# Two more pairs as seven block products in two feed-forward networks, small filler products and another GpSimd order at the head

## The chip, the cores and the metric

The kernel runs on one core of one Trainium2 chip. The metric is the device time of one execution in microseconds (us). The page of the profile names the engines of the core by short names: PE is TensorE, which multiplies matrices (PEld is its loading of weights), DVE is VectorE, ACT is ScalarE, POOL is GpSimd, and SP is the engine that does little but start transfers.

## What is computed

The reference is a trunk of two layers on 512 tokens of width 1024. Each layer is a feed-forward network, an attention mixer and a second feed-forward network, each behind a normalisation that is shifted, scaled and gated by columns computed from a conditioning vector `c`:

```python
for i in range(DEPTH):                      # 2
    mod = silu(c) @ mod_w[i] + mod_b[i]     # nine vectors of 1024
    sh1, sc1, g1, sh2, sc2, g2, sh3, sc3, g3 = jnp.split(mod, 9, axis=-1)
    h = modulate(rms_norm(x), sh1, sc1)
    x = x + 0.5 * g1[:, None, :] * swiglu(h, ffn1_w_gu[i], ffn1_w_down[i])
    h = modulate(rms_norm(x), sh2, sc2)
    x = x + g2[:, None, :] * mixer(h)       # sparse attention, then forgetting attention
    h = modulate(rms_norm(x), sh3, sc3)
    x = x + 0.5 * g3[:, None, :] * swiglu(h, ffn2_w_gu[i], ffn2_w_down[i])
    x = rms_norm(x, post_gain[i])
```

`swiglu` multiplies `h` by a gate matrix and an up matrix of 1024 x 2816, forms `silu(gate) * up`, and multiplies by a down matrix. All of it is float32.

## The kernel before

**Tiles.** The 512 tokens lie along the free dimension, the features on partitions. A weight matrix comes as units of 128 output features: one unit is a tile of 128 x 1024 (8 blocks of 128 x 128). Each unit is loaded by SP into one of four slots of `wraw`, split by ACT into a rounded part `whi` (line 664 or 675) and by DVE into the rest `wlo` (line 1125 or 1131), and multiplied by TensorE in three products: `whi` by the rounded activations, `wlo` by the rounded ones, `whi` by their rest. 

**The four networks.** They are numbered f = 0 to 3. A network goes in three thirds of 8, 8 and 6 pairs. A pair is a gate unit and an up unit of the same 128 hidden features; after the pairs of a third come 8 down units. A **plain pair** is 2 units x 8 blocks x 3 products = 48 matmuls of 512 columns (lines 1862, 1863, 1867). A **summed pair** takes the 2 x 2 blocks of the two units and of the activations and forms seven block products instead of eight: 7 x 4 blocks x 3 products = 84 matmuls of 256 columns (lines 1942 to 1944, `sum_pair` on PE). `PLAIN_PAIRS` says how many pairs of each third stay plain; all others are summed.

**What a summed pair asks of the other engines.** DVE adds and subtracts the weight blocks in `combine` (lines 1149 to 1154) for the pair that comes next, splits its four groups (`group_lo`, line 1131), and puts the partial sums together (lines 1192, 1195, 1201). ACT rounds the groups (`group_hi`, line 675) and copies partial sums out of PSUM before TensorE writes the bank again: `keep_one` (line 702), and in `sum_pair` the two, five and three (lines 719, 721, 724). TensorE's seventh product waits for the copy of line 724 (`three_kept`). On ACT that copy stands behind the rounding of group 1 of the next pair, and this rounding waits for the third of the four instructions of DVE's `combine` for that pair (line 1152).

**Before the first summed pair of a network** DVE also forms four differences of the activations (`diff_t`, line 1166), which ACT rounds and DVE splits (`split_t`, line 1172); `T_ROUND_AT` and `T_SPLIT_AT` say after which plain pair. In network 2 DVE also scales the result of layer 0 in eight instructions (`post_first`, line 1463), placed by `POSTS_AT`; they read a PSUM bank that the summed pairs use, so TensorE waits for all eight (`pe.wait_ge(posted, KT)`) ahead of the first summed pair.

**The columns.** `mod` is computed on DVE, one tile of 128 x 1024 at a time (`mod_column`, line 1215). `MOD_PLACES` lists for each network after which pair (third, 0, pair) or which down unit (third, 1, unit) a tile is done. GpSimd fetches the tiles into a few slots (`fetch`, `late_place`).

**Order.** There is no scheduler. Each engine runs its instructions in the order in which its block of the program issues them, and waits on counters. On DVE the loop over the plain pairs of a network issues, for pair n: the product of gate and up (line 1486), the split of the weights of pair n + 2, or, if that is the first summed pair, its `combine` and two groups, the rest of the hidden tile (line 1498), then what the tables place there: the splits of the differences, the columns, the scalings. DVE's `sum_pair` begins with the `combine` of the next pair.

**The head.** TensorE spreads the conditioning vector (line 2134), sums squares (line 2138) and spreads the root (line 1952), with waits in between, in `first_stat`. Then `first_units` multiplies the first four units, block by block, as DVE (line 1609), ACT (lines 776 and 779) and GpSimd (line 561) finish each of the 8 blocks of the normalised activations: for each block units 0 and 1, then units 2 and 3 of the block before. GpSimd also splits the weights of units 2 and 3 (`first_lo`, line 553).

## Time and profile before

| | |
|---|---|
| median of 3 runs | 1936.67 us (1932.82 to 1937.36) |
| the profiled execution | 1936.46 us |
| its span in the trace | 1934.7 us |
| PE busy | 1903.3 us (98%) |
| DVE busy | 1508.9 us (78%) |
| ACT busy | 967.6 us (50%) |
| POOL busy | 212.5 us (11%) |

The span is the time from the first to the last instruction of the program; 1.8 us of the execution lie around it. PE's busy time counts matmuls that overlap each other in the pipeline, so it does not tell how fast they follow one another; the starts of the instructions do. A row of the timeline begins with its start and its duration in us; where instructions of one kind follow without a gap they are merged, and xN gives their number. In square brackets stands how long the engine had been idle before and what ended it. The granted clock (PEclk) is 1.00 at 2.4 GHz and 0.50 at 1.2 GHz.

### The profile page before, as it was taken

How to read it: one execution, taken by the hardware profiler on the slowest of the kernel's cores; microseconds unless marked ns; L12 is line 12 of the kernel's file. 1: busy time of each engine (PE TensorE's matmuls, PEld its weight loads, DVE VectorE, ACT ScalarE, POOL GpSimd, SP SyncE). 2: the span in 40 equal slices, each digit the busy share in tenths (PEclk: the TensorE clock that was granted, in tenths of full speed). 3: DMA queues.
4: the chain of work that ended last, by engine and by line, in shares of the span. 5: the costliest groups of instructions: out<-in, count | busy, mean ns of one | idle time of the engine just before them, and what ended most of it. 6: DMA issues, size and time to landing. Idle time of an engine off the chain costs nothing.

```text
span 1934.7 us, 29256 instructions
## 1 busy us (share of the span) xinstructions
PE 1903.3 (98%) x11364; PEld 1690.3 (87%) x11364; DVE 1508.9 (78%) x2264; ACT 967.6 (50%) x1556; POOL 212.5 (11%) x245
## 2 busy tenths in 40 slices
PE   6999999999999999999999999999999999999998
PEld 5789989888888889899888999977888889899897
DVE  7889888699868798897888988785555478578485
ACT  5324626464746436346542653655565456356264
POOL 3110000016710020000011000001101000000000
PEclk9999999999999999999999999999999999999999
DMA  8775352322053583633267443323223232323232
GB/s 336 275 277 188 123 174 92 119 88 88 23 163 120 187 287 115 224 110 103 80 207 258 164 147 116 109 88 115 88 91 95 61 98 83 125 87 120 77 101 75
DMA packets 76411, 264.84 MB, mean 137 GB/s; under 512 B 8897, under 2 KB 11073, under 8 KB 76274
## 3 DMA queue, kind: packets, MB, share of 16 engines
q1 hardware_dynamic: 55296, 190.34, 30.3%
q0 software_dynamic: 20256, 72.02, 10.8%
q8 instruction: 91, 1.49, 0.3%
q10 hardware_dynamic: 722, 0.61, 0.1%
q14 instruction: 46, 0.38, 0.1%
HBM read 260.66 MB, written 2.13 MB: 136 GB/s over the span
## 4 chain that ended last, share of the span: by engine, by line
PE 88%; DVE 7%; issue 1%; DMA 1%; POOL 1%; ACT 1%; SPq 0%; DVEq 0%; ACTq 0%; POOLq 0%
PE bank L1862 17%; PE bank L1867 16%; PE bank L1863 16%; PE bank L1943 11%; PE bank L1942 11%; PE bank L1944 11%; DVE arena L1679 1%; DVE arena L1215 1%; DVE top L1678 1%; PE bank L2348 1%; PE bank L2365 1%; PE bank L2280 1%; PE bank L2124 1%; DVE h_lo L1395 1%; DVE wlo L1125 1%
## 5 line engine op out<-in xcount | busy, mean ns | idle before, releaser
L1862 PE MATMUL bank<-hid_hi,whi 128*128 128x512 f32 (+1 forms) x856 | 328.8, 384 | 0.0
L1863 PE MATMUL bank<-hid_hi,wlo 128*128 128x512 f32 (+1 forms) x856 | 328.0, 383 | 0.0
L1867 PE MATMUL bank<-hid_lo,whi 128*128 128x512 f32 (+1 forms) x856 | 328.0, 383 | 0.0
L1862 PE MATMUL bank<-h_hi,whi 128*128 128x512 f32 x784 | 313.4, 400 | 5.2 <-ACT h_hi L779 2.8
L1863 PE MATMUL bank<-h_hi,wlo 128*128 128x512 f32 x784 | 307.1, 392 | 0.0
L664 ACT ACTIVATE whi<-wraw 128x1024 fp32r<-128x1024 f32 x210 | 219.4, 1053 | 150.1 <-PE bank L1867 129.6
L1942 PE MATMUL bank<-h_hi,whi 128*128 128x256 f32 x1024 | 289.9, 283 | 0.5 <-ACT sq L724 0.5
L1943 PE MATMUL bank<-h_hi,wlo 128*128 128x256 f32 x1024 | 289.7, 283 | 0.0
L1944 PE MATMUL bank<-h_lo,whi 128*128 128x256 f32 x1024 | 289.7, 283 | 0.0
L1125 DVE TENSOR_TENSOR wlo<-wraw,whi 128x1024 fp32r<-128x1024 f32 x196 | 238.2, 1223 | 58.6 <-ACT whi L664 58.2
L1867 PE MATMUL bank<-h_lo,whi 128*128 128x512 f32 x784 | 279.4, 393 | 3.1 <-POOL h_lo L561 3.0
L1943 PE MATMUL bank<-mix,wlo 128*128 128x256 f32 x768 | 217.2, 283 | 0.0
L1944 PE MATMUL bank<-mix,whi 128*128 128x256 f32 x768 | 217.0, 283 | 0.0
L1942 PE MATMUL bank<-mix,whi 128*128 128x256 f32 x768 | 215.5, 281 | 0.0
L675 ACT ACTIVATE whi<-arena 128x1024 fp32r<-128x1024 f32 x128 | 135.2, 1056 | 137.9 <-PE bank L1944 56.1
L1131 DVE TENSOR_TENSOR wlo<-arena,whi 128x1024 fp32r<-128x1024 f32 x128 | 156.6, 1224 | 54.1 <-ACT whi L675 53.8
L1942 PEld LDWEIGHTS bank<-h_hi,whi 128*128 128x128 f32 x1024 | 196.3, 192 | 1.5 <-ACT sq L724 0.7
L1943 PEld LDWEIGHTS bank<-h_hi,wlo 128*128 128x128 f32 x1024 | 196.2, 192 | 0.4
L1944 PEld LDWEIGHTS bank<-h_lo,whi 128*128 128x128 f32 x1024 | 196.3, 192 | 0.0
L1867 PEld LDWEIGHTS bank<-hid_lo,whi 128*128 128x128 f32 x856 | 160.8, 188 | 31.7
L1862 PEld LDWEIGHTS bank<-hid_hi,whi 128*128 128x128 f32 x856 | 160.9, 188 | 31.0
L1863 PEld LDWEIGHTS bank<-hid_hi,wlo 128*128 128x128 f32 x856 | 160.9, 188 | 30.9
(294 smaller groups left out, 3353.7 us busy)
## 6 DMA issues: line engine op xcount, KB each, us to landing
wraw<-in_w_units_dram SPq DMA_DIRECT2D x306, 512.0 KB, 3.8
arena<-in_mod_t_dram POOLq DMA_DIRECT2D x96, 512.0 KB, 5.2
mod_tile<-in_mod_t_dram POOLq DMA_DIRECT2D x32, 512.0 KB, 5.5
wraw<-in_w_units_dram SPq DMA_DIRECT2D x32, 384.0 KB, 3.2
arena<-in_w_units_dram SPq DMA_DIRECT2D x10, 512.0 KB, 4.3
arena<-in_mod_t_dram SPq DMA_DIRECT2D x7, 512.0 KB, 5.9
xT<-in_xt_dram SPq DMA_DIRECT2D x8, 256.0 KB, 4.2
sq<-k_roots POOLq DMA_DIRECT2D x8, 256.0 KB, 3.7
```

The lines of the kernel that those rows point to most:

```text
L664: act.activation(whi[:, s % RING, :, :], wraw[:, s % RING, :, :], ACT.Copy).then_inc(hi_ready, 1)
L675: act.activation(split_group(whi, s, g), weight_group(s, g), ACT.Copy)\
L1125: dve.tensor_tensor(wlo[:, s % RING, :, :], wraw[:, s % RING, :, :], whi[:, s % RING, :, :].bitcast(F32), ALU.subtract).then_inc(lo_ready, 1)
L1131: dve.tensor_tensor(split_group(wlo, s, g), weight_group(s, g), split_group(whi, s, g).bitcast(F32), ALU.subtract).then_inc(lo_ready, GROU ...
L1215: dve.tensor_tensor_reduce(out=src, in0=src, in1=cond_wide if t < MOD_FIRST else cond[:, :], scale=1.0, scalar=cols[:, col:col + 1], op0=A ...
L1395: dve.scalar_tensor_tensor(out=h_lo[:, k, :], in0=normal(k), scalar=modc[:, base + k:base + k + 1], in1=h_hi[:, k, :].bitcast(F32), op0=AL ...
L1862: pe.matmul(dst, whi[:, w, k, :], hi_, start=first, stop=False)
L1863: pe.matmul(dst, wlo[:, w, k, :], hi_, start=False, stop=False)
L1867: return pe.matmul(dst, whi[:, s % RING, k, :], lo_, start=False, stop=last)
L1942: pe.matmul(dst, w_hi[:, at, :], m_hi, start=p in (0, 1, 3) and k == 0, stop=False, skip_group_check=True)
L1943: pe.matmul(dst, w_lo[:, at, :], m_hi, start=False, stop=False, skip_group_check=True)
L1944: ins = pe.matmul(dst, w_hi[:, at, :], m_lo, start=False, stop=k == 3, skip_group_check=True)
```

## The change

In networks 1 and 2 the first third keeps 4 plain pairs instead of 6, so 18 of 22 pairs are summed instead of 16 (network 3 is already so). The tables that place DVE's work move with it: the differences are rounded and split by pair 3, the eight scalings of network 2 stand after pairs 0, 1 and 2, and the columns of the first third after pairs 2 and 3. Network 1 does 5 columns there instead of 6, network 2 does 4 instead of 6; the others go to down units of the second third. The slots of the fetched tiles (`late_place`) and GpSimd's waits in `fetch` follow the new numbers. At the head TensorE gets 40, 36 and 36 small products (identity by the mask, 128 columns, bfloat16) after the spread vector, after the sums and after the spread root; their result in bank 3 is overwritten. GpSimd splits unit 2 after block 0 and unit 3 after block 1, instead of both after block 0.

```diff
-              [None] * KT + [(0, 0, n) for n in (3, 3, 3, 4, 4, 4)]
+              [None] * KT + [(0, 0, n) for n in (2, 2, 3, 3, 3)]
...
-              + [(1, 1, d) for d in (0, 0, 0, 1, 1, 1, 2, 3, 3, 4, 5, 5, 7, 7)],
-              [(0, 0, n) for n in (3, 3, 3, 4, 4, 4)] + [(0, 1, d) for d in (0, 0, 0, 1, 1, 1, 2, 2, 2, 3, 3, 3, 4, 4, 5, 5, 6, 6, 7, 7)]
-              + [(1, 1, d) for d in (0, 0, 0, 1, 1, 1)], []]
+              + [(1, 1, d) for d in (0, 0, 0, 1, 1, 1, 2, 3, 3, 4, 4, 5, 5, 7, 7)],
+              [(0, 0, n) for n in (2, 3, 3, 3)] + [(0, 1, d) for d in (0, 0, 0, 1, 1, 1, 2, 2, 2, 3, 3, 3, 4, 4, 5, 5, 6, 6, 7, 7)]
+              + [(1, 1, d) for d in (0, 0, 0, 1, 1, 1, 2, 2)], []]
...
-PLAIN_PAIRS = {0: (8, 0, 0), 1: (6, 0, 0), 2: (6, 0, 0), 3: (4, 0, 0)}
+PLAIN_PAIRS = {0: (8, 0, 0), 1: (4, 0, 0), 2: (4, 0, 0), 3: (4, 0, 0)}
...
-        T_ROUND_AT = {0: {0: (0, 1, 2), 6: (3,)}, 1: {0: (0, 1, 2), 4: (3,)}, 2: {0: (0, 1, 2), 4: (3,)}, 3: {0: (0, 1, 2), 2: (3,)}}
-        T_SPLIT_AT = {0: {2: (0, 1, 2), 7: (3,)}, 1: {1: (0, 1), 2: (2,), 5: (3,)}, 2: {1: (0, 1), 2: (2,), 5: (3,)}, 3: {1: (0, 1, 2), 3: (3,)}}
-        POSTS_AT = {0: (0,), 2: (1, 2, 3), 3: (4, 5, 6, 7)}
+        T_ROUND_AT = {0: {0: (0, 1, 2), 6: (3,)}, 1: {0: (0, 1, 2), 2: (3,)}, 2: {0: (0, 1, 2), 2: (3,)}, 3: {0: (0, 1, 2), 2: (3,)}}
+        T_SPLIT_AT = {0: {2: (0, 1, 2), 7: (3,)}, 1: {1: (0, 1, 2), 3: (3,)}, 2: {1: (0, 1, 2), 3: (3,)}, 3: {1: (0, 1, 2), 3: (3,)}}
+        POSTS_AT = {0: (0,), 1: (1, 2, 3), 2: (4, 5, 6, 7)}
...
-                if k == 1:
-                    first_lo(2)
-                    first_lo(3)
+                if k in (1, 2):
+                    first_lo(k + 1)
...
+            def clock_keeping(n):
+
+                for _ in range(n):
+                    pe.matmul(bank[3][:, 0:P], ident_b[:, :], causal[:, :], start=True, stop=True)
...
                 ins.then_inc(cond_spread, 1)
+                clock_keeping(40)
                 pe.wait_ge(first_added, KT - 1)
...
                 ins.then_inc(stat_done, 1)
+                clock_keeping(36)
                 pe.wait_ge(root_ready, 1)
                 spread(bank[RB], 0, 0).then_inc(rb_ready, 1)
+                clock_keeping(36)
```

Lines of the changed kernel stand 5 higher than before on DVE and up to 6 higher on POOL (DVE's column is line 1215 before and 1220 after).

DVE in network 1, around the change from the plain pairs to the summed ones. `hid_lo` is the rest of the last plain pair's hidden tile, `wlo<-wraw` the last group of the first summed pair, `h_lo<-arena` the fourth split of the differences, ISA is `mod_column` (its second row only writes the column), and `arena<-wraw` is the first instruction of the `combine` for the second summed pair. Before:

```order
L1498 TENSOR_TENSOR hid_lo<-dve_tmp,hid_hi 128x512 [waits hid_rounded]
L1131 TENSOR_TENSOR wlo<-wraw,whi 128x512 [waits hi_ready]
L1172 TENSOR_TENSOR h_lo<-arena,h_hi 128x4x256 [waits t_rounded]
L1149 TENSOR_TENSOR arena<-wraw 128x512 [waits raw_in0,raw_in3,lo_ready]
L1150 TENSOR_TENSOR arena<-wraw 128x512
L1152 TENSOR_TENSOR arena<-arena,wraw 128x512 [waits w_combined]
```

After, in the same place:

```order
L1503 TENSOR_TENSOR hid_lo<-dve_tmp,hid_hi 128x512 [waits hid_rounded]
L1136 TENSOR_TENSOR wlo<-wraw,whi 128x512 [waits hi_ready]
L1177 TENSOR_TENSOR h_lo<-arena,h_hi 128x4x256 [waits t_rounded]
L1220 ISA mod_tile,modc<-mod_tile,cond,cols 128x1024 [waits ring_in3]
L1220 ISA modc 128x1
L1220 ISA arena,modc<-arena,cond,cols 128x1024 [waits ring_in4]
L1220 ISA modc 128x1
L1220 ISA arena,modc<-arena,cond,cols 128x1024 [waits ring_in0]
L1220 ISA modc 128x1
L1154 TENSOR_TENSOR arena<-wraw 128x512 [waits raw_in0,raw_in3,lo_ready]
```

Three columns now stand between the last split and the `combine` of the second summed pair, where none stood.

DVE in network 2, from the rest of a hidden tile on. L1463 before and L1468 after is `post_first`; the product of gate and up is L1486 and L1491. Before, after plain pair 3 of 6:

```order
L1498 TENSOR_TENSOR hid_lo<-dve_tmp,hid_hi 128x512 [waits hid_rounded]
L1215 ISA arena,modc<-arena,cond,cols 128x1024 [waits ring_in1]
L1215 ISA modc 128x1
L1215 ISA arena,modc<-arena,cond,cols 128x1024 [waits ring_in2]
L1215 ISA modc 128x1
L1215 ISA mod_tile,modc<-mod_tile,cond,cols 128x1024 [waits ring_in3]
L1215 ISA modc 128x1
L1463 SCALAR_TENSOR_TENSOR xT<-xT,cols,bank 128x512 x4
L1486 TENSOR_TENSOR dve_tmp<-act_tmp,bank 128x512 [waits act_out]
L1149 TENSOR_TENSOR arena<-wraw 128x512 [waits raw_in2,raw_in1,lo_ready]
```

After, from pair 2 of 4 on:

```order
L1503 TENSOR_TENSOR hid_lo<-dve_tmp,hid_hi 128x512 [waits hid_rounded]
L1220 ISA arena,modc<-arena,cond,cols 128x1024 [waits ring_in1]
L1220 ISA modc 128x1
L1468 SCALAR_TENSOR_TENSOR xT<-xT,cols,bank 128x512 x4
L1491 TENSOR_TENSOR dve_tmp<-act_tmp,bank 128x512 [waits act_out]
L1136 TENSOR_TENSOR wlo<-arena,whi 128x1024 [waits hi_ready]
L1503 TENSOR_TENSOR hid_lo<-dve_tmp,hid_hi 128x512 [waits hid_rounded]
L1136 TENSOR_TENSOR wlo<-wraw,whi 128x512 [waits hi_ready]
L1177 TENSOR_TENSOR h_lo<-arena,h_hi 128x4x256 [waits t_rounded]
L1220 ISA arena,modc<-arena,cond,cols 128x1024 [waits ring_in2]
```

The last four scalings moved from behind pair 3, with the `combine` of the first summed pair still to come, to behind pair 2, with that `combine` already done; two more plain pairs used to follow them, now one product does.

POOL at the head. `h_lo<-arena` is the rest of one block of the activations, `wlo<-wraw` a `first_lo`. Before:

```order
L545 TENSOR_TENSOR rstd<-var,minus_half 128x4 [waits var_ready]
L561 TENSOR_TENSOR h_lo<-arena,h_hi 128x512 [waits h_rounded]
L553 TENSOR_TENSOR wlo<-wraw,whi 128x1024 [waits lo_ready,hi_ready] x2
L561 TENSOR_TENSOR h_lo<-arena,h_hi 128x512 [waits h_rounded] x7
L530 DMA arena<-in_mod_t_dram 128x1024 [waits mod_done] x2
```

After:

```order
L551 TENSOR_TENSOR rstd<-var,minus_half 128x4 [waits var_ready]
L566 TENSOR_TENSOR h_lo<-arena,h_hi 128x512 [waits h_rounded]
L559 TENSOR_TENSOR wlo<-wraw,whi 128x1024 [waits lo_ready,hi_ready]
L566 TENSOR_TENSOR h_lo<-arena,h_hi 128x512 [waits h_rounded]
L559 TENSOR_TENSOR wlo<-wraw,whi 128x1024 [waits lo_ready,hi_ready]
L566 TENSOR_TENSOR h_lo<-arena,h_hi 128x512 [waits h_rounded] x6
```

Block 1 of the activations now goes ahead of the weights of unit 3.

## Rows read from the trace of the kernel before

**Rows 1.** The page: busy time of each engine, share of the span, instructions.

```profile
PE 1903.3 (98%) x11364; PEld 1690.3 (87%) x11364; DVE 1508.9 (78%) x2264; ACT 967.6 (50%) x1556; POOL 212.5 (11%) x245
```

**Rows 2.** Windows: stretch, length, busy (x instructions) by engine, clock, DMA, GB/s.

```profile
603.87:647.41 43.54, 43.54 (x193) 36.04 (x192) 33.07 (x41) 17.48 (x23) 4.30 (x8) 1.00 0.52 164
711.26:791.84 80.58, 80.58 (x673) 80.57 (x672) 70.10 (x97) 50.49 (x86) 2.12 (x4) 1.00 0.46 149
1620.66:1661.10 40.44, 40.44 (x337) 40.33 (x336) 34.30 (x46) 27.37 (x46) 0.00 (x0) 1.00 0.39 120
```

**Rows 3.** Timeline, network 3, first summed pair from 1620.66: DVE, ACT, PE.

```profile
1621.56 0.69 DVE L1486 TENSOR_TENSOR dve_tmp<-act_tmp,bank 128x512 f32<-128x512 f32 x1 [2.96 <-ACT act_tmp L801]
...
1625.99 0.69 DVE L1149 TENSOR_TENSOR arena<-wraw 128x512 f32<-128x512 f32 x1
...
1627.96 1.06 ACT L675 ACTIVATE whi<-arena 128x1024 fp32r<-128x1024 f32 x1 [0.97 <-DVE arena L1152]
...
1628.92 0.37 ACT L724 ACTIVATE sq<-bank 128x256 f32<-128x256 f32 x1
...
1629.16 0.28 PE L1944 MATMUL bank<-h_lo,whi 128*128 128x256 f32 x1
...
1629.34 0.39 PE L1942 MATMUL bank<-h_hi,whi 128*128 128x256 f32 x1
```

**Rows 4.** Timeline, DVE, network 1: two columns that follow each other.

```profile
630.31 1.28 DVE L1215 CUSTOM_DVE_ANT_0 arena<-arena,cond,cols 128x1024 f32<-128x1024 f32 x1
...
631.51 1.28 DVE L1215 CUSTOM_DVE_ANT_0 arena<-arena,cond,cols 128x1024 f32<-128x1024 f32 x1
```

**Rows 5.** Timeline, network 2: DVE's work, and PE's fifth pair.

```profile
970.17 2.35 DVE L1125 TENSOR_TENSOR wlo<-wraw,whi 128x1024 fp32r<-128x1024 f32 x2
...
974.18 2.06 DVE L1463 SCALAR_TENSOR_TENSOR xT<-xT,cols,bank 128x512 f32<-128x512 f32 x3
...
978.03 0.39 PE L1862 MATMUL bank<-h_hi,whi 128*128 128x512 f32 x1
...
986.30 2.72 DVE L1463 SCALAR_TENSOR_TENSOR xT<-xT,cols,bank 128x512 f32<-128x512 f32 x4
...
990.41 0.69 DVE L1149 TENSOR_TENSOR arena<-wraw 128x512 f32<-128x512 f32 x1
...
995.29 0.68 DVE L1498 TENSOR_TENSOR hid_lo<-dve_tmp,hid_hi 128x512 fp32r<-128x512 f32 x1
```

**Rows 6.** Windows, as in rows 2: where the granted clock falls and stays low.

```profile
22.30:25.70 3.40, 1.19 (x4) 0.70 (x4) 3.37 (x6) 1.35 (x2) 3.26 (x3) 1.00 1.05 418
27.18:32.72 5.54, 5.54 (x15) 4.30 (x13) 5.50 (x10) 2.71 (x4) 2.71 (x3) 0.50 0.96 337
1316.20:1319.40 3.20, 1.66 (x13) 1.32 (x11) 2.50 (x4) 2.80 (x4) 1.10 (x2) 1.00 0.18 50
1319.40:1322.80 3.40, 3.40 (x11) 2.40 (x10) 3.40 (x8) 2.72 (x6) 0.00 (x0) 0.52 0.85 233
```

**Rows 7.** Timeline of the head: PE, DVE and POOL.

```profile
10.79 1.87 PE L2138 MATMUL bank<-ones,ssum 128*128 128x1 f32 x8 [2.86 <-DVE ssum L1599]
...
13.06 0.15 DVE L1238 TENSOR_SCALAR var<-bank 128x4 f32<-128x4 f32 x1
...
19.22 0.76 PE L1862 MATMUL bank<-h_hi,whi 128*128 128x512 f32 x1 [2.47 <-ACT h_hi L779]
...
20.41 4.89 POOL L553 TENSOR_TENSOR wlo<-wraw,whi 128x1024 fp32r<-128x1024 f32 x2
...
26.59 1.22 PE L1867 MATMUL bank<-h_lo,whi 128*128 128x512 f32 x2 [2.99 <-POOL h_lo L561]
...
41.46 1.29 POOL L561 TENSOR_TENSOR h_lo<-arena,h_hi 128x512 fp32r<-128x512 f32 x1 [1.89 <-ACT h_hi L779]
...
50.54 0.50 PE L1862 MATMUL bank<-h_hi,whi 128*128 128x512 f32 x1 [1.31 <-DVE wlo L1125]
```

**Rows 8.** Timeline, PE, forgetting attention: the product with the mask, and the next.

```profile
1318.37 0.23 PE L2359 MATMUL bank<-causal,ident_b 128*128 128x128 bf16 x1
1318.41 0.36 PE L2124 MATMUL bank<-mix 128*128 128x256 f32 x1
```

More of the change, by code:

```diff
@@ L233, in late_place, with late_three @@
             m = t - late_first(t)
-            return m % 3 if m < 6 else (m - 6) % 4
+            n = late_three(t)
+            return m % 3 if m < n else (m - n) % 4
+        def late_three(t):
+            return 4 if t >= FFN_TILES[2] else 5
         front_slot = late_slot + [piece(4 * D, D), piece(5 * D, D)]
@@ L532, in fetch @@
             def fetch(t):
-                m, n = t - late_first(t), 6
+                m, n = t - late_first(t), late_three(t)
                 if FFN_TILES[1] <= t < FFN_TILES[1] + KT:
                     m = n
-                pool.wait_ge(mod_done, max(t - (0 if m == 0 else 2 if 3 <= m < n + 3 else MOD_RING - 1), MOD_FIRST))
-                if m in (0, n + 3):
+                pool.wait_ge(mod_done, max([u + 1 for u in range(late_first(t), t) if late_place(u) == late_place(t)], default=late_first(t))
+                             if t >= FFN_TILES[1] + KT else t - MOD_RING + 1)
+                if t >= FFN_TILES[1] + KT and m in (0, n + 3):
                     pool.wait_ge(t_split, 4 * sum(t >= FFN_TILES[f] for f in (1, 2)) + (4 if m else 3))
@@ L2126, in score @@
                 return pe.matmul(dst, q_lo, k_hi, start=False, stop=last)
+            def clock_keeping(n):
+                for _ in range(n):
+                    pe.matmul(bank[3][:, 0:P], ident_b[:, :], causal[:, :], start=True, stop=True)
             def first_stat():
                 pe.wait_ge(const_ready, 6)
+                pe.wait_ge(bf_ready, 1)
                 pe.wait_ge(silu_ready, 1)
```

## The prediction

> **What bounds the kernel now.** I read the page first: PE is busy 98% of the span, DVE 78% [rows 1]. Since its matmuls overlap, I then took their starts from the windows. Four plain pairs (192 matmuls, 193 with the one that straddles the edge) fill 43.54 us, 226.8 ns each; eight summed pairs (672) fill 80.58 us, 119.9 ns each [rows 2]. Nothing stands between them: PE's stream is closed from 50.54 us on, apart from some gaps of 1 to 2 us [rows 7]. So a column saved on PE is time saved, and a wait put into PE is time lost, one for one. The exception is the head, where PE waits for DVE, ACT and GpSimd and runs at half its clock. Last I read the timelines of DVE, ACT and PE where plain pairs turn into summed ones, since the change moves this place by 21.8 us of PE's time and the other engines must be ready that much earlier.
>
> **Four pairs become summed.** A plain pair takes 48 x 226.8 ns = 10.89 us, a summed one 84 x 119.9 ns = 10.07 us [rows 2]. Each pair gives 0.81 us; two in each of two networks give **-3.3 us**. The columns fall by an eighth, the time by a thirteenth, because a matmul of half the columns costs more than half. The Trainium skill (TensorE: Matmul & The Clock Gate, Back-to-back issue gap) gives N/2.4 + 2.5 ns for a matmul of N columns, 215.8 and 109.2 ns here; by that the four pairs would give 4.8 us and the sum would be 1.5 us lower. The trace does not agree, and the rows decide.
>
> **Network 1: three columns in a chain without slack.** Network 3 has already 4 plain pairs. There the first summed pair starts at 1620.66 [rows 2]; DVE begins the combine for the second one at 1625.99; ACT's rounding of its group 1 starts at 1627.96, released by the third instruction of that combine; ACT's copy for the seventh product follows at 1628.92; and PE starts that product at 1629.34, 0.18 us after the matmul before it where 0.12 is the rule [rows 3]. So the product started at the very moment it could: no slack. In network 1 the change puts three columns, 1.20 us each from start to start [rows 4], right before that combine. The two columns after pair 2 cost nothing: DVE idles 2.96 us in that place of network 3 [rows 3] and 2 x 1.2 fit. The three after pair 3 have no cover. Combine, rounding and copy each come 3.6 us later, and PE stands still **+3.6 us** in front of the seventh product. After that product PE and DVE are about where network 3 has them, so I charge the delay once.
>
> **Network 2: the scalings.** PE may not start the first summed pair before all eight scalings are done. In the kernel before they end at 986.30 + 2.72 = 989.0, when two plain pairs are still to run. After, PE reaches this point when its fourth plain pair ends, at 978.03 [rows 5]. DVE's work up to there: before, the scalings 1 to 3 end at 974.18 + 2.06 = 976.24. The change takes the two splits for pair 4 out (2.35, of which 2.27 advance the queue) and puts in the combine with two groups, 995.29 - 990.41 = 4.88. That gives 976.24 - 2.27 + 4.88 = 978.85. One column (1.2) and four scalings (2.72) follow: 982.8. DVE has hardly any idle time in this stretch that could take it up. PE waits 982.8 - 978.0 = **+4.8 us**. Then three columns stand before the second combine here too. DVE comes to them a little earlier relative to the pair, as its product L1486 starts with the pair and not 0.9 us behind it, while the tile's rounding still waits for ACT's copy after product one: **+3.4 us** instead of 3.6.
>
> **The clock after these waits.** Two stretches of the trace show what a standing PE costs. With 1.19 us busy in 3.4 the granted clock fell and was 0.50 until 32.7, and after a stretch with 1.66 in 3.2 it was 0.52 for 3.4 us [rows 6]. At half clock 3.4 us lose 1.7. All three new waits are as long as those or longer. I take 1.5 for network 1. In network 2 the first loss is mostly covered by the second wait, which runs on DVE's and ACT's time, so I take 1.0 for both. Together **+2.5 us**, with ends of 0 (no drop) and 6.8 (two stretches of 6.8 us at half clock lose 3.4 each).
>
> **The head.** From 27.18 to 32.72 PE's matmuls followed one another at 5.54 / 13 = 0.43 us (13 weight loads) at a clock of 0.50 [rows 6], against 0.227 at full clock. Two things are changed. GpSimd's order: both weight splits took 4.89 us from 20.41 on, and the rest of block 1 came so late that PE waited 2.99 us until 26.59 [rows 7]. After, block 1 is done near 24.2 (20.41 + 2.45 + 1.29), but unit 3's weights only near 26.6, so PE goes on without a break at the same 26.6, with 84 instead of 86 matmuls left. The fillers: the one product like them in the trace starts 0.04 us before the next matmul at full clock [rows 8]; I take that and, for half clock and a queue of nothing else, 0.11 as ends. From 10.79 - 2.86 = 7.9 on forty end between 9.5 and 12.3; the sums behind them (1.87) must be done when DVE wants them at 13.06 [rows 7], so they delay DVE by 0 to 1.1. The next 36 and the last 36 lie in waits of about 2 us each and fit at full clock only. What they can bring is bounded by data: the last rest of block 7 lands at 41.46 + 1.29 = 42.75 [rows 7], 2 + 12 matmuls follow, 45.9; before, the units ended 1.31 ahead of 50.54, at 49.2 [rows 7]. So at best -3.3, and the gain passes on, since the next pair's start follows the units through ACT and DVE. But behind the last filler PE has only 12 matmuls (2.7 us at full clock) in the 7.4 us from 19.22 to 26.6 [rows 7], about the share at which the clock fell [rows 6]. I expect it low again at 26.6 and 3 to 6 us after, which leaves 0.4 to 2.2: **-1.3 us**. If the fillers themselves run at half clock to the end (3.9 us a batch), they hold up the spread and the first unit: +2.7.
>
> The Trainium skill (TensorE: Matmul & The Clock Gate, What's actually happening) says that the low clock is the default and activity lifts it; fillers are activity. By that alone the head would give its whole 3.3 and the sum would be 2.0 lower. No row here shows fillers at work.
>
> **What costs nothing.** The moved columns: network 1 gets one more behind down unit 4, network 2 two behind unit 2. DVE's splits there run some units ahead of PE; without that cover they would cost 1.2 us each. GpSimd's new waits release a tile's fetch earlier or at the same time. Transfers take about 5 us, and the tiles of pair 3 can be fetched when those of pair 2 are done.
>
> **Sum** against the profiled execution, 1936.46 us (0.2 below the median): -3.3 + 3.6 + 4.8 + 3.4 + 2.5 - 1.3 = +9.7, **1946.2 us**.
>
> **The rivals.** (1) The cover holds, and the kernel is faster. That needs DVE to reach the second combine by 5.3 us after the first summed pair's start, and the last scaling by the end of plain pair 3, in both networks. Then the waits and their clock losses are gone: -3.3 - 1.3 = -4.6, 1931.9, or 1929.9 with the whole head gain. For it speaks only that DVE is busy 78% of the span; against it, that DVE's order is fixed and the sums above leave 3 to 5 us open. It decides from the point at which the waits in all are below 4.6 us. (2) The clock stays up. The fillers lift it, the units run at full clock from 19.22 on, and it survives the new waits too: -3.3 + 11.8 - 3.3 = +5.2, 1941.7. Against it stand the 12 matmuls in 7.4 us and the two falls [rows 6]. The Trainium skill's rule on the default clock (the page and section above) is on its side. (3) The fillers stay at half clock and delay the chain at the head: +2.7 instead of -1.3, 1950.2; against it, that they are the densest work PE has there. (4) The summed pairs don't do what they say: no reason, since networks 1 to 3 already run 50 of them at 10.07 us.
>
> **How the numbers follow.** A measurement of this kernel can tell about 0.3% (5.8 us) from no change, so 1930.9 to 1942.5 counts as no change. The forecast has 0.70, and its own range is 1941.5 (no clock loss, the head at -2.2, the three waits 1.3 shorter in all) to 1951.5 (5 more from the clock and the head). Rival 1 has 0.09, rival 2 0.14, rival 3 0.07. The range reaches to rival 2 and takes in most of rival 3: 1939 to 1951.5. Slower: all of the forecast but 0.05, rival 3, and a third of rival 2 for the clock in a wait: 0.77. No change: 0.05, most of rival 2, some of rival 1: 0.15. Faster: 0.08.
>
> **What would show it.** In the profile after: summed pairs of 10.07 us; a gap in PE of about 3.6 us in front of the seventh product of the first summed pair of networks 1 and 2, released by ACT's line for the three-copy, with three columns ahead of the combine on DVE; a gap of about 4.8 us ahead of network 2's first summed pair, ended by a scaling; a granted clock of 0.5 behind these gaps; units of the head that end between 46 and 49 us. It is wrong if these gaps are below 1.5 us each, or if the head gains or loses more than 3.3.

## The result, and the profile after

The changed kernel takes 1945.72 us (median of 4 runs, 1944.56 to 1947.21), beside 1935.93 us of the kernel before in the same session. The ratio is 1.0061, with an interval from 1.0049 to 1.0073: slower, by 9 to 14 us. The two medians alone differ by 9.8 us (1.0051), near the lower end of that interval. The profiled execution took 1944.56 us, its span is 1942.8.

The page of the profile after, busy time by engine (compare [rows 1]):

```profile
PE 1907.2 (98%) x11620; PEld 1702.3 (88%) x11620; DVE 1528.4 (79%) x2296; ACT 981.3 (51%) x1584; POOL 211.7 (11%) x245
```

Shares of busy time hide the whole matter: PE is busy 98% before and after. The waits by line, of PE in networks 1 and 2 (waited for, total us, times, longest), show it. Before:

```profile
PE bank L1952 <- DVE root L1231: 0.7, 1, 0.7
PE bank L1942 <- ACT sq L724: 0.5, 1, 0.5
```

After:

```profile
PE bank L1947 <- ACT sq L729: 6.7, 2, 3.5
PE bank L1947 <- DVE xT L1468: 4.5, 1, 4.5
PE bank L1957 <- DVE root L1236: 0.7, 1, 0.7
```

The first two rows are the three waits of the forecast: two for ACT's copy ahead of a seventh product (before, the same copy was waited for once, 0.5 us, near 1072), one for a scaling. Now the place in network 1, as [rows 3] showed it for network 3: columns, `combine`, rounding, copy, seventh product.

```profile
628.37 1.28 DVE L1220 CUSTOM_DVE_ANT_0 mod_tile<-mod_tile,cond,cols 128x1024 f32<-128x1024 f32 x1
...
629.58 1.28 DVE L1220 CUSTOM_DVE_ANT_0 arena<-arena,cond,cols 128x1024 f32<-128x1024 f32 x1
...
630.78 1.28 DVE L1220 CUSTOM_DVE_ANT_0 arena<-arena,cond,cols 128x1024 f32<-128x1024 f32 x1
...
631.99 0.68 DVE L1154 TENSOR_TENSOR arena<-wraw 128x512 f32<-128x512 f32 x1
...
633.96 1.06 ACT L680 ACTIVATE whi<-arena 128x1024 fp32r<-128x1024 f32 x1 [4.58 <-DVE arena L1157]
634.93 0.37 ACT L729 ACTIVATE sq<-bank 128x256 f32<-128x256 f32 x1
...
631.55 0.28 PE L1949 MATMUL bank<-h_lo,whi 128*128 128x256 f32 x1
635.34 0.58 PE L1947 MATMUL bank<-h_hi,whi 128*128 128x256 f32 x1 [3.52 <-ACT sq L729]
```

From the start of the `combine` to the seventh product it is 635.34 - 631.99 = 3.35 us. In [rows 3] it is 1629.34 - 1625.99 = 3.35 as well. So whatever delays the `combine` reaches PE undiminished. PE stands 3.79 us from start to start, 3.67 more than the 0.12 of the rule.

Network 2 has both waits (PE's timeline; in the last row 997.07 - 993.62 = 3.45):

```profile
978.47 0.61 PE L1872 MATMUL bank<-h_lo,whi 128*128 128x512 f32 x2
983.59 0.58 PE L1947 MATMUL bank<-h_hi,whi 128*128 128x256 f32 x1 [4.51 <-DVE xT L1468]
...
993.62 0.28 PE L1949 MATMUL bank<-h_lo,whi 128*128 128x256 f32 x1
997.07 0.58 PE L1947 MATMUL bank<-h_hi,whi 128*128 128x256 f32 x1 [3.17 <-ACT sq L729]
```

The granted clock in and behind the three waits (windows: stretch, length, PE busy, clock, DMA share, GB/s):

```profile
631.70:635.20 3.50, 0.13 (x2) 1.00 0.68 224
635.30:638.70 3.40, 3.36 (x15) 0.50 0.91 340
638.70:642.10 3.40, 3.40 (x31) 1.00 0.68 201
978.90:983.40 4.50, 0.18 (x1) 1.00 0.19 43
983.50:986.90 3.40, 3.31 (x15) 0.51 0.35 117
993.80:997.00 3.20, 0.10 (x1) 1.00 0.45 140
997.10:1000.50 3.40, 3.40 (x16) 0.50 1.00 396
```

Behind each wait 15 or 16 matmuls (those cut by an edge counted too) fill a stretch that holds 31 at full clock: half clock for 3.4 us.

To see where the time went, I cut the span at the points where PE begins to spread the root of a normalisation. The stages of the profiled executions, in us:

| stage | before | after | difference |
|---|---|---|---|
| head and network 0 | 384.01 | 382.81 | -1.20 |
| sparse attention | 202.53 | 201.13 | -1.40 |
| network 1 | 352.66 | 356.11 | +3.45 |
| network 2 | 349.79 | 358.38 | +8.59 |
| forgetting attention | 292.61 | 290.83 | -1.78 |
| network 3 | 339.23 | 339.24 | 0.0 |

The end behind network 3 is 0.4 longer; with it the differences add up to the span's 8.1.

The -1.78 is not the change's. In the 14 profiled executions of this study the stage lasts either 290.3 to 291.1 or 292.6 to 292.9, with the edits and without; the execution before was one of the four upper ones. These four have a stretch of 3.4 us at half clock there [rows 6], the ten others have none. The -1.40 was not in the forecast; it has a section of its own below.

### The profile page after: what moved, and what is told of

Same layout as the page of the kernel before. It is cut to its first block, busy times and chain, and to the rows that moved or that the text cites. A ratio compares the mean times of both kernels' runs of the same rounds, so it can differ in the third digit from the quotient of the medians.

```text
span 1942.8 us, 29880 instructions
## 1 busy us (share of the span) xinstructions
PE 1907.2 (98%) x11620; PEld 1702.3 (88%) x11620; DVE 1528.4 (79%) x2296; ACT 981.3 (51%) x1584; POOL 211.7 (11%) x245
## 4 chain that ended last, share of the span: by engine, by line
PE 92%; DVE 4%; issue 1%; ACT 1%; POOL 1%; DMA 1%; SPq 0%; DVEq 0%; ACTq 0%; POOLq 0%
PE bank L1867 17%; PE bank L1872 17%; PE bank L1868 17%; PE bank L1948 12%; PE bank L1947 12%; PE bank L1949 12%; PE bank L2362 1%; PE bank L2379 1%; PE bank L2294 1%; PE bank L2129 1%; DVE h_lo L1400 1%; PE bank L2131 1%; PE bank L2130 1%; DVE dve_tmp L1409 0%; PE bank L2351 0%
## 5 line engine op out<-in xcount | busy, mean ns | idle before, releaser
L1947 PE MATMUL bank<-h_hi,whi 128*128 128x256 f32 x1088 | 310.3, 285 | 11.2 <-ACT sq L729 6.7
L1948 PE MATMUL bank<-h_hi,wlo 128*128 128x256 f32 x1088 | 309.8, 285 | 0.0
L1949 PE MATMUL bank<-h_lo,whi 128*128 128x256 f32 x1088 | 309.6, 285 | 0.0
L1867 PE MATMUL bank<-h_hi,whi 128*128 128x512 f32 x720 | 287.2, 399 | 6.5 <-ACT h_hi L784 2.5
L1868 PE MATMUL bank<-h_hi,wlo 128*128 128x512 f32 x720 | 281.2, 391 | 0.0
L1872 PE MATMUL bank<-h_lo,whi 128*128 128x512 f32 x720 | 258.4, 391 | 0.7 <-POOL h_lo L566 0.5
L1949 PE MATMUL bank<-mix,whi 128*128 128x256 f32 x816 | 230.5, 282 | 0.0
L1947 PE MATMUL bank<-mix,whi 128*128 128x256 f32 x816 | 228.8, 280 | 0.0
L1947 PEld LDWEIGHTS bank<-h_hi,whi 128*128 128x128 f32 x1088 | 210.8, 194 | 12.5 <-ACT sq L729 7.1
L1948 PEld LDWEIGHTS bank<-h_hi,wlo 128*128 128x128 f32 x1088 | 210.6, 194 | 0.4
L1949 PEld LDWEIGHTS bank<-h_lo,whi 128*128 128x128 f32 x1088 | 210.7, 194 | 0.0
```

What stands on the lines that cost most here:

```text
L1867: pe.matmul(dst, whi[:, w, k, :], hi_, start=first, stop=False)
L1868: pe.matmul(dst, wlo[:, w, k, :], hi_, start=False, stop=False)
L1872: return pe.matmul(dst, whi[:, s % RING, k, :], lo_, start=False, stop=last)
L1947: pe.matmul(dst, w_hi[:, at, :], m_hi, start=p in (0, 1, 3) and k == 0, stop=False, skip_group_check=True)
L1948: pe.matmul(dst, w_lo[:, at, :], m_hi, start=False, stop=False, skip_group_check=True)
L1949: ins = pe.matmul(dst, w_hi[:, at, :], m_lo, start=False, stop=k == 3, skip_group_check=True)
```

## Experiment 1: the head alone, the pairs alone, and the two halves of the head

Four kernels: before with both edits of the head, after without them, before with the fillers alone, before with GpSimd's order alone. The edits:

```diff
-                if k == 1:
-                    first_lo(2)
-                    first_lo(3)
+                if k in (1, 2):
+                    first_lo(k + 1)
...
+                clock_keeping(40)
...
+                clock_keeping(36)
```

Head alone: 

> The kernel before with the head's edits alone (fillers, GpSimd's order); the networks keep 6 plain pairs. My theory: the head gives what the profile of after shows up to the start of the second pair, 1.2 us (49.33 instead of 50.54), and up to 0.7 more, because in that execution DVE's first additions came 0.66 later by a wait for ACT's squares that the change does not touch; so 1934.0 to 1935.0 beside 1936 of the kernel before. Rival: the further 1.4 us that after had gained by 576.7 us is the head's too (later engines shifted against each other), then 2.6 to 3.3 us faster, 1932.8 to 1933.4.

Pairs alone: 

> The changed kernel without the head's edits: four more summed pairs and the moved columns, scalings and splits. My theory: pairs -3.3, three waits of 3.7, 4.7 and 3.3, the clock 4.5: +12.9 by the sum of the gaps, less up to 1.8 for a clock drop at 1319 us that the execution of after did not have; so 1946.5 to 1948.5. Rival: the gain after the head (1.4 us up to 576.7) belongs to the pairs; then the time is near that of the whole change plus 1.2, at most 1947, and the first part of the profile up to 576.7 shows the gain without the head's edits.

Fillers alone: 

> The kernel before with the fillers alone, GpSimd in the old order. My theory: PE still waits for GpSimd until about 26.6 us; the fillers lift the clock earlier and shorten the stretch at half clock from 5.5 to about 3.4 us, so 0.5 to 1.2 us faster. Rival: the old wait of 3 us is what lets the clock fall; it falls after the wait as before and the fillers bring nothing (within 0.3 us).

Order alone: 

> The kernel before with GpSimd's other order alone, no fillers. My theory: two of 88 matmuls leave the half-clock stretch, the rest follows as before, 0 to 0.5 us faster. Rival: the order is the whole gain, because the longest wait is split in two; then 1.0 to 1.5 us faster and a shorter stretch at half clock.

These texts count from 1936 us, and the kernel before took 1933.48 beside these runs, so the comparison goes by the differences and ratios.

| kernel | median us | ratio to before (interval) | head and network 0 | sparse attention |
|---|---|---|---|---|
| before, same session | 1933.48 | | | |
| head alone | 1931.69 | 0.9989 (0.9980 to 0.9997) | 382.30 | 201.16 |
| fillers alone | 1932.59 | 0.9996 (0.9987 to 1.0005) | 384.06 | 201.12 |
| order alone | 1932.38 | 0.9994 (0.9985 to 1.0003) | 382.21 | 202.46 |
| pairs alone | 1948.07 | 1.0073 (1.0061 to 1.0086) | 382.93 | 202.49 |

The head alone is faster, by 0.6 to 3.9 us. That covers its theory (1 to 2) and its rival (2.6 to 3.3); its stages show that the rival's further 1.4 us are there (201.16 in the sparse attention). The two halves can't be told from no change by their times, but their stages are told apart. With GpSimd's new order the head and network 0 last 382.1 to 382.8 us in all ten profiled executions that have it (mean 382.4). With the old order they last 384.01, 382.93, 384.06 and 383.10 (the last from experiment 4), mean 383.5, with or without fillers. So by the means the order brings about 1.2 us, and the fillers nothing at this place (384.06 beside 384.01 with the old order, 382.30 beside 382.21 with the new). My theory for the halves had it the wrong way round; the rival of the order kernel, that it is the whole gain, stands. With four executions of the old order the size is rough. Two of them had half clock for 6.8 us near 28 us (384.01 and 384.06), two for 3.4 (382.93 and 383.10). Beside the three executions with the new order and the same 3.4 us at half clock (382.21, 382.37, 382.81), the order brings about 0.5; the rest of the 1.2 goes with the longer half clock, which none of the ten with the new order had.

GpSimd's rows in the kernel after show the order at work (compare the row of 20.41 in [rows 7], where both weight splits stand together):

```profile
21.07 2.37 POOL L559 TENSOR_TENSOR wlo<-wraw,whi 128x1024 fp32r<-128x1024 f32 x1
23.41 1.27 POOL L566 TENSOR_TENSOR h_lo<-arena,h_hi 128x512 fp32r<-128x512 f32 x1
24.65 2.37 POOL L559 TENSOR_TENSOR wlo<-wraw,whi 128x1024 fp32r<-128x1024 f32 x1
```

What did the fillers do, then? They brought the full clock earlier. Without them the first units' products follow one another at 0.43 us up to 22.4 us or later (19.78, 20.21, 20.63 in the kernel before); in the kernel after they follow at 0.24 from 20.18 on. The half clock near 28 us also became rarer: it came in all three kernels without fillers, in the one with forty of them (experiment 4), and in three of the ten with all of them (the kernel after, the fillers alone, network 1's columns moved). But with the new order the stage is no shorter where it stayed away (382.1 to 382.5 in seven executions) than where it came. PE only waits longer for its next block, here before and after:

```profile
22.40 0.49 PE L1862 MATMUL bank<-h_hi,whi 128*128 128x512 f32 x1 [0.29 <-ACT h_hi L779]
23.06 0.47 PE L1867 MATMUL bank<-h_hi,whi 128*128 128x512 f32 x1 [1.16 <-ACT h_hi L784]
```

The fillers' own rate differed. In the kernel after the first 25 or so of the forty start 107 ns apart, the last ones 56. In three others (the first try with the scalings, filled waits, everything moved) 65 or more products start 107 apart. With everything moved:

```profile
7.87 4.45 PE L2142 MATMUL bank<-causal,ident_b 128*128 128x128 bf16 x40
13.78 3.64 PE L2142 MATMUL bank<-causal,ident_b 128*128 128x128 bf16 x36
17.23 1.09 PE L1962 MATMUL bank<-ident_r,root 128*128 128x128 f32 x8
```

So the spread of the root comes at 17.2 us in these three and at 15.1 to 15.4 in the seven others that have all fillers. Yet the pair behind the first units starts at 48.9 to 49.0 in the three, and at 48.6 to 49.3 in the others (50.5 with the fillers alone).

The pairs alone cost 12 to 17 us, 14.6 by the medians. The prediction's terms without the head add up to 11.0, just under that interval: right in kind, a little small, as the clock's term is (see below). Its sparse attention lasts 202.49, so the -1.40 isn't the pairs'; the rival falls.

## Experiment 2: take away what makes PE wait, one cause at a time

The first two kernels move columns, with everything else as in the changed kernel. Network 1's go behind the last pairs of the network, network 2's behind summed pairs of its second third, where DVE's loop was given a line for them:

```diff
-              [None] * KT + [(0, 0, n) for n in (2, 2, 3, 3, 3)]
+              [None] * KT + [(0, 0, n) for n in (2, 2)]
...
-              + [(1, 1, d) for d in (0, 0, 0, 1, 1, 1, 2, 3, 3, 4, 4, 5, 5, 7, 7)],
+              + [(1, 1, d) for d in (0, 0, 0, 1, 1, 1, 2, 3, 3, 4, 4, 5, 5, 7, 7)] + [(2, 0, n) for n in (4, 5, 5)],
```

```diff
-              [(0, 0, n) for n in (2, 3, 3, 3)] + [(0, 1, d) for d in (0, 0, 0, 1, 1, 1, 2, 2, 2, 3, 3, 3, 4, 4, 5, 5, 6, 6, 7, 7)]
+              [(0, 0, n) for n in (2,)] + [(0, 1, d) for d in (0, 0, 0, 1, 1, 1, 2, 2, 2, 3, 3, 3, 4, 4, 5, 5, 6, 6, 7, 7)] + [(1, 0, n) for n in (5, 7, 7)]
```

Network 1: 

> The changed kernel; network 1's three columns ahead of the second combine stand behind the last two summed pairs of the network instead, where DVE idles. My theory: the gap of 3.8 us before the seventh product of network 1's first summed pair falls to 0.1 to 0.2, and the half clock behind it (3.4 us, loses 1.7) goes too: 5.4 us less than the changed kernel, about 1940.3. Rival: DVE or ACT was late there for another reason (the splits pulled forward), and a gap of over 1 us stays; or the columns cost in their new place what they cost in the old; then 1943 to 1946.

It took 1939.88 us, beside 1932.94 of before (1.0034, 1.0021 to 1.0047). No wait is left in network 1, and the stage lasts 351.03 us: 5.08 less than after, and 1.63 less than before. This is the whole gain of two pairs, 2 x 0.81 = 1.62. Network 1's loss is the three columns and nothing else.

Network 2: 

> The changed kernel; network 2's three columns ahead of the second combine stand behind later summed pairs (one behind the sixth, two behind the eighth of the second third). My theory: the second gap of network 2 (3.45 us before the seventh product) goes with its half clock (1.7): 5.0 us less than the changed kernel, about 1940.7; the first gap of 4.9 stays. Rival: DVE is late by the scalings, not by the columns; then the second gap stays at 2 us or more, and the time at 1943.5 or above.

It took 1941.03 us (1.0039, 1.0024 to 1.0054). The second wait of network 2 is gone (between the first and 1199 us no start-to-start is over 0.4 us), the first stays at 4.95. The stage lasts 354.82, 3.56 less than after: the wait's 3.33, and little more, since a new wait of 1.46 us near 1199 took back part of what the clock gave.

The scalings. The spread that they read was put into a bank that no summed pair writes, four of them behind the summed pairs, and PE's wait, until then ahead of the summed pairs, behind them:

```diff
-        POST_RB = 4
+        POST_RB = 7
...
-        POSTS_AT = {0: (0,), 1: (1, 2, 3), 2: (4, 5, 6, 7)}
+        POSTS_AT = {0: (0,), 1: (1, 2, 3), 4: (4,), 5: (5,), 6: (6,), 7: (7,)}
...
-                        if f == 2 and t == 0:
-                            pe.wait_ge(posted, KT)
                         for n in range(PLAIN_PAIRS[f][t], k):
                             sum_pair(up + 2 * n, f if up + 2 * n == first_sum(f) else None)
+                        if f == 2 and t == 0:
+                            pe.wait_ge(posted, KT)
```

> The changed kernel; the spread that the eight scalings of network 2 read lies in a bank that no summed pair writes, PE waits for the scalings only behind the third's pairs, and scalings 4 to 7 stand one behind each summed pair. My theory: the first gap of network 2 (4.9 us) falls to 0.1, its half clock (about 1.7) with it, the second gap of 3.3 stays, since DVE waits there for PE's first product anyway: 6 us less than the changed kernel, 1939 to 1940.5. Rival: DVE has no room; the second gap grows by what the first loses, or each of the four scalings lengthens its summed pair by up to 0.7; then 1942.5 or more.

It took 1946.84 us (1.0073, 1.0058 to 1.0088): not better than the changed kernel. The first wait is gone, but there is a new one behind the eighth summed pair. PE's timeline in this kernel:

```profile
1025.13 0.28 PE L1952 MATMUL bank<-h_lo,whi 128*128 128x256 f32 x1
1029.45 0.50 PE L1870 MATMUL bank<-hid_hi,whi 128*128 128x512 f32 x1 [4.03 <-DVE xT L1468]
```

L1468 is the last scaling. DVE does it at the very end of its work for the eighth pair, and I had put PE's wait right there. The wait had only moved. The next kernel moves it ahead of the next third's pairs:

> As the first try with the scalings (own bank, one behind each summed pair), but PE waits for them only ahead of the next third's pairs, so that the last one, which comes behind the eighth summed pair, holds nobody up. My theory: the gap of 4.3 us behind the eighth summed pair goes; the first gap of network 2 stays away, the second stays at 4.1 (with half clock behind it): about 5 us less than the changed kernel, a ratio of 1.003 to 1.004 to the kernel before. Rival: the down products then wait for DVE for another reason; a gap of over 2 us stays behind the eighth summed pair and the ratio is 1.005 or more.

It took 1941.16 us (1.0043, 1.0029 to 1.0057), and the 4.3 us are gone. The second wait of network 2 stays (4.11 from start to start), as both texts expected; network 2 lasts 354.31, 4.07 less than after. The ratio is somewhat above what I wrote (1.003 to 1.004); a wait of 1.38 us near 1201 that the kernel after does not have is part of it, and 0.8 us of longer half clock in network 1 (see experiment 3).

## Experiment 3: leave the waits and keep the clock

Rival 2 of the prediction said that the clock might stay up behind the waits. Here all three waits stay, and PE does small products in them:

```diff
+                            clock_keeping(70, OB)
                             pe.wait_ge(posted, KT)
...
+                        if f in (1, 2):
+                            clock_keeping(55 if f == 1 else 50, OB)
                         pe.wait_ge(three_kept, n + 1)
```

> The changed kernel with small filler products in its three new waits (55 in network 1, 70 and 50 in network 2, into a bank that nothing reads then); the waits themselves stay. My theory: the waits are as long as before, but the granted clock stays at 1.0 behind them, which gives back what the half clock cost: 1.7 + 1.7 + 1.1, 4.5 us, about 1941.2. Rival: the clock falls all the same, as it did at 27.7 us behind the head's fillers, and the time stays at 1945 to 1946; or the fillers still run when the wait ends and cost up to 0.5 each.

It took 1941.31 us (1.0042, 1.0025 to 1.0059). PE's timeline and windows in this kernel:

```profile
631.31 3.24 PE L2140 MATMUL bank<-causal,ident_b 128*128 128x128 bf16 x55
634.98 0.39 PE L1949 MATMUL bank<-h_hi,whi 128*128 128x256 f32 x1 [0.43 <-ACT sq L729]
```

```profile
635.00:638.40 3.40, 3.40 (x28) 1.00 0.85 329
...
981.80:985.20 3.40, 3.40 (x28) 1.00 0.37 110
...
994.10:997.50 3.40, 3.40 (x29) 1.00 0.97 392
```

The seventh product comes 3.80 us after the sixth's last matmul (634.98 - 631.18), as without fillers. But the clock is 1.00 behind all three. Network 1 lasts 354.64 (1.47 less than after), network 2 356.08 (2.30 less). So the clock behind the waits costs 3.8 us in all, a third of what the waits themselves cost.

Is the fall certain after such a wait? No. Over the kernels of this study there are 15 unfilled waits of 2.8 to 5.0 us, 14 in these places and one behind the eighth summed pair. Behind 14 the clock fell. Behind one, network 1 of the kernel with network 2's columns moved, it did not, though the wait was the same 3.79 us and PE as idle:

```profile
631.10:634.60 3.50, 0.11 (x1) 1.00 0.72 193
634.80:638.20 3.40, 3.40 (x29) 1.00 0.99 382
```

Network 1 lasts 354.65 there, the same as with filled waits. Nor is the fall always of one length. In the kernel with the scalings' late wait the clock fell during the wait of network 1, and PE had half clock for 5.2 us behind it:

```profile
634.70:639.90 5.20, 5.20 (x24) 0.50 0.77 277
```

The five kernels with the unfilled wait of 3.79 us in network 1 last 354.65, 355.97, 356.11, 356.14 and 356.92 us there: the same wait cost 0 to 2.3 us of clock. What decides it is open.

## Experiment 4: the 1.4 us in the sparse attention

The stage lasts 202.5 us in before, in the order alone and in the pairs alone, and 201.1 in every kernel with fillers, though these lie 400 us earlier. In the trace of before PE waits near 490 us for DVE's masking, and DVE is late from its products with the roots of the keys on, which GpSimd stores and reads back, and which come late. Three answers for the kernel before: transfers between 436.0 and 442.5 us (a queue's packets, MB and share; an issue's KB and us to landing), DVE's products with the roots, PE's wait.

```profile
q8 instruction: 1, 0.02, 1.4%
...
k_roots<-rstd POOLq DMA_DIRECT2D x1, 4.0 KB, 3.7
```

```profile
446.61 3.57 DVE L1693 TENSOR_TENSOR arena<-arena,mix 128x512 f32<-128x512 f32 x2 [0.41 <-DMA mix<-k_roots]
```

```profile
491.87 0.33 PE L2124 MATMUL bank<-mix,hid_hi 128*128 128x128 f32 x1 [1.07 <-DVE rowmax L1552]
```

A packet of code is under way beside the 4 KB store. In half-microsecond steps from the store's issue it lies between 1.0 and 1.5 us in the kernel before, in the order alone and in the pairs alone, and there the store takes 3.7, 3.8 and 3.5 us. In the ten kernels with all the fillers the packet comes 5.0 us or more behind the issue (in one 1.5 to 2.0 ahead of it), and the store takes 2.0 to 2.2. The fillers put 112 more products into PE's code, so a packet comes at another time. That queue q8 carries PE's code is read from its count, which goes with PE's matmuls: 91 packets at 11364 of them (before), 92 at 11476 (the fillers alone), 93 at 11620 (after), 94 at 11795 (filled waits). To try this without the head's other effects, I put 40 fillers in front of the first sums, in a wait, and nothing else:

```diff
                 ins.then_inc(cond_spread, 1)
+                clock_keeping(40)
                 pe.wait_ge(first_added, KT - 1)
```

> The kernel before with 40 fillers ahead of the first sums, and nothing else: at the head they lie in a wait, but every later instruction of PE stands 80 places further back in its code. In the three programs without fillers one packet of code was under way beside the 4 KB store of the roots, near 439 us, and the store took 3.5 to 3.8 us; in the seven with fillers no packet was there and it took 2.0 to 2.2. My theory: with the code moved the packet comes at another time, the store takes 2.0 us and PE's wait of 1.1 us near 490 goes; about 1.3 us faster, though the head is as it was. Rival: the store is faster because of what the fillers do at the head (clock, order of the engines); 40 fillers ahead of the sums change nothing of that, the store takes 3.7 and the time is that of the kernel before.

It took 1932.05 us, beside 1933.51 (0.9993, 0.9984 to 1.0002). The time alone does not settle it, the trace does. No instruction packet lies between 2 us before and 7 us behind the issue, and:

```profile
k_roots<-rstd POOLq DMA_DIRECT2D x1, 4.0 KB, 2.1
```

```profile
445.30 2.12 DVE L1693 TENSOR_TENSOR arena<-arena,mix 128x512 f32<-128x512 f32 x2
```

PE's wait near 490 is gone, and the stage lasts 201.18 us. At the head these forty did nothing for the clock (it fell near 27 us, and the stage's 383.10 is among the old order's). So the fillers' only measured gain has nothing to do with the clock: they shift the code.

The late store alone does not explain the 1.4. Counted from the stage's start, DVE's two products start 0.1 to 0.8 us later in the three kernels with the late store, and the second takes 2.2 us instead of 1.1 (3.57 for both in the row above, 2.12 in the last one). In the kernel before GpSimd is at work beside it (from 447.54 us on), and DVE's second product starts at 448.0; in the eleven others it starts ahead of that work. That the two engines hold each other up is argued from this, not tried. Likewise, that the packet itself holds up the store is argued from their going together in all 14 traces; the packet alone was not tried.

## Experiment 5: everything moved

Network 1's and network 2's columns and the scalings as in experiment 2 (with the late wait), the head as in the change. A second kernel adds 18 fillers in each of the two longest waits between the head's first units.

> The changed kernel with all three waits' causes moved: network 1's three columns behind its last two summed pairs, network 2's three behind summed pairs of its second third, the spread for the scalings in a bank of its own, scalings 4 to 7 one behind each summed pair, and PE's wait for them ahead of the next third's pairs. My theory: what is left is the pairs' -3.3 and the head's -1.8, so 4 to 5.5 us faster than the kernel before (a ratio of 0.9972 to 0.9979), and no gap of PE over 1.2 us in networks 1 and 2. Rival: the moved columns and scalings cost in their new places 0.5 to 1 each (seven places), then -1.5 to +1 us.

> As the kernel with everything moved, with 18 more fillers in each of the two longest waits between the first units (1.6 and 2.0 us). My theory: the granted clock does not fall between 24 and 33 us; it had fallen there in the changed kernel and in the one with fillers alone, but not in the one with the head's edits alone, so the gain is between 0 and 1.2 us. Rival: the first units' end is set by the blocks that ACT and GpSimd hand over every 3.19 us, and the fillers bring nothing or delay the units by up to 0.5.

They took 1929.89 and 1929.57 us, beside 1933.51 of before: 0.9986 (0.9977 to 0.9995) and 0.9981 (0.9972 to 0.9990). Both beat the kernel before and the changed one. All waits of PE in networks 1 and 2 of the first:

```profile
PE bank L1952 <- ACT sq L729: 0.9, 3, 0.5
PE bank L1962 <- DVE root L1236: 0.7, 1, 0.7
```

Network 1 gives its whole 1.6 (351.04). Network 2 lasts 349.28, beside 348.98 to 349.83 in the kernels with its six plain pairs: its gain is used up by small waits, of 0.50, 0.45 and 0.81 us from start to start. The first is the seventh product of the first summed pair again. DVE's `combine` starts at 979.53 there and the product at 982.88, 3.35 later; DVE still comes 0.4 too late. By the medians the gain is 3.6 us, a little below the 4 to 5.5 that I expected, and it came from the head, the shifted code and one network. The extra fillers brought no clear difference: the intervals overlap, and the clock did not fall near 28 us in the kernel without them either.

## Why the prediction was right, step by step

The forecast was 1946.2 us, with a range of 1939.0 to 1951.5; 1945.72 were measured. The mechanism was right in the networks, where nearly all of the time lies; at the head it was wrong. By its terms:

- **Pairs, -3.3.** Network 1 with its columns moved gives 1.63 us for two pairs: right to 0.02. The two rates of [rows 2] were the right basis, not the count of columns.
- **Network 1's wait, +3.6.** 3.67. Right, mechanism and size; moving the columns removes it.
- **Network 2's wait for the scalings, +4.8.** From start to start PE lost 4.67 (4.90 less the 0.23 of a plain matmul). Right. One reading beside the sum was wrong: when the scalings of the kernel before ended at 989.0, PE had one plain pair left, not two (978.03 + 10.89 = 988.92 by [rows 5] and [rows 2]).
- **Network 2's second wait, +3.4.** 3.33. Right. It depends on PE's own start, as I had argued: it came to 4.1 when the first wait was gone.
- **The clock, +2.5.** Right in kind, mis-sized: 3.8 by experiment 3, of it 1.5 in network 1 as forecast, and 2.3 in network 2 where I had taken 1.0. I had reasoned that the second wait would cover the first loss. It does not: from the first product to the seventh of that summed pair it is 13.48 us after (983.59 to 997.07) and 12.27 with filled waits (981.75 to 994.02). The first loss passes on for 1.2, because ACT in turn waits for PE's first product: its copy of it starts 2.97 us after that product's start in the kernel after (986.56) and 1.74 with filled waits (983.49), and DVE's next work waits for ACT.
- **The head, -1.3.** -1.2, but by the order alone, so the size is luck. The step that failed is the fillers': I let both edits share the gain through the clock. The fillers lifted the clock as I had hoped (see experiment 1), and the stage was not shorter for it. Rival 3's delay came in three kernels (the spread of the root at 17.2 us), and it did not reach the next pair, where the rival had +2.7.
- **What costs nothing.** The columns that the change moved to the second third cost nothing that shows.

Missing in the sum was the shifted code, -1.4. It and the under-sized clock term (+1.3) cancel by luck, which is why the sum comes closer than its parts deserve. Of the rivals, the first fell with the waits. The second, that the clock stays up, came true in one wait of 15. The third's delay came in three of the ten kernels with all fillers and cost nothing that shows. The Trainium skill (TensorE: Matmul & The Clock Gate, What's actually happening) says that activity releases the low clock. The filled waits agree (1.00 behind three of three), and so does the head (107 ns between fillers, then 56); but at the head the earlier full clock gave no time, since PE waited for its blocks.

## What to carry to other kernels

Where one engine is busy without a break, look at the others' queues at the places where its kind of work changes: work that fitted into two more plain pairs had no cover when these became summed, and 3.3 us of gain brought 11.7 us of waits. Measure once how long the chain is from the helper engine's first instruction to the main engine's need (3.35 us here, in networks 1 and 3 and in the kernel with everything moved); then any work put in front of it can be priced before it is run. If a wait on the main engine can't be avoided, filling it with small products gave back the part that the clock takes (three waits of three here).

## What I had not expected of the hardware

- A 4 KB store took 3.5 to 3.8 us where a packet of code followed it by 1.0 to 1.5 us, and 2.0 to 2.2 elsewhere. Forty products in the head, which cost nothing there, moved the code and gained 1.4 us some 480 us later.
- The granted clock fell behind 14 of 15 waits of 2.8 to 5.0 us, and stayed at 1.00 behind one. Behind the same wait of 3.79 us the loss was 0 to 2.3 us in five kernels: the 1.5 of the kernel after is a likelihood, not a constant.
- Small products in the head's waits brought the full clock some 10 us earlier in the kernel after, and the time there did not change: PE waited longer for its blocks.
